# Second matrices of the wide layer: 512-column products made as two of 256 columns, and the row tiles moved by 128 bytes

## The chip, the cores and the metric

One core of a Trainium2 chip runs the whole program. The metric is the device time in microseconds. The kernel before took 1237.65 us (median of three runs, 1237.44 to 1240.28).

## What is computed

The reference runs four layers over 256 positions of width 1024: an SSM layer, an attention layer, and two layers of a second block. Each layer of the second block ends in a wide (feed-forward) part with a hidden width of 2816:

```python
h = rms_norm_2(x, ln_ffn_pre[l])
f = (jax.nn.silu(h @ ffn_w_gate[l]) * (h @ ffn_w_up[l])) @ ffn_w_down[l]
x = x + rms_norm_2(f, ln_ffn_post[l])
```

The change touches `@ ffn_w_down[l]`, a product of 256 x 2816 by 2816 x 1024, once for each of two layers.

## The kernel before

All weights come as one stream of slots. A slot holds up to two k-tiles (128 rows of a matrix each) of one chunk, and a chunk is 512 columns wide in most matrices. SP issues one DMA for each slot into `weights_raw`. ACT rounds the slot to `weights_hi` (fp32r), DVE makes `weights_lo` = raw - hi, and TensorE forms each product as hi*hi + hi*lo + lo*hi, so three matmuls stand for one. The activations are split the same way: `act_F_hi`/`act_F_lo` for most matrices, `ffn_F_hi`/`ffn_F_lo` (22 k-tiles of 256 positions) for the down matrix.

There are two forms of this triple:

- **Rows held** (`tile_slot`, lines 705 to 707). 128 positions of the activation rows are the stationary operand (the weight load reads 128 of them) and 512 columns of the weight slot stream through. It is called for each of the two tiles of positions, writes `acc[par][t]`, a PSUM bank of 512 columns, and is used by nearly all matrices. Two chunks are 416 columns wide and four are 384, and their matmuls are as wide.
- **Weights held** (`hidden_slot`, lines 683 to 685). 128 columns of the weight slot are stationary and 256 positions of the activations stream through. It is used for the last two attention input chunks, the convolution input, and chunks 1 to 10 of the gate and up matrices of the wide layer.

The order on TensorE is written out by hand. In each wide layer it is: chunk 0 of gate/up with rows held, chunks 1 to 10 with weights held (960 matmuls, after the first 96 of which four transposes are put in), and then the down matrix: `down.0` slot by slot, `down.1` with seven slots so and the last four tile by tile (`by_tile(4, {})`). The down matrix has 22 k-tiles x 2 tiles of positions x 2 chunks x 3 = 264 matmuls of 512 columns for each layer. After it ACT squares the result (line 1284), POOL makes the root and DVE normalises.

SBUF tiles are placed in the order of the `sb(...)` calls, one after another, and some tiles lie over others that are dead by then. Between them stand unused tiles whose only effect is a shift. By these sizes `weights_hi`, `weights_lo` and their `_more` pairs begin 192 bytes past a multiple of 256. `act_F_*`, `mla_F_*`, `conv_F_*`, `attn_F_*` and `ffn_F_*` begin 128 bytes past one. A k-tile of 512 columns is 2048 bytes of a partition and one of 384 columns 1536, both multiples of 256. One of 416 columns is 1664 bytes, so the second k-tile of such a slot begins 64 bytes past a multiple of 256.

Of the kernel before, what the change touches and what calls it, by code (L numbers as in the profile page):

```python
# [8 lines left out]
F32 = mybir.dt.float32  # L9
# [6 lines left out]
P = 128  # L16
# [158 lines left out]
def build(nc, stream, consts, x_in, ssm_ab, ssm_ldt, ssm_bc, rows, qk_gain, positions, decay, conv_p, lat_gain, out):  # L175
# [17 lines left out]
    with ctx:  # L193
        def sb(name, shape, dt=F32, scope=None):
            return (scope or ctx).enter_context(nc.sbuf_tensor(name, shape, dt))
# [32 lines left out]
        for a in begins:  # L228
            for p in range(R, R + R_MORE):
                n = min(n for n in range(a + R, NS) if place[n] == p)  # L230
# [37 lines left out]
        with ExitStack() as s1:  # L268
# [4 lines left out]
            par = sb("ssm_par", [P, 20, Q], F32, s1)  # L273
# [43 lines left out]
            ao_lo = sb("attn_F_lo", [P, HEADS, SEQ], F32R, s2)  # L317

        with ExitStack() as s3:
            h2_hi = sb("ffn_F_hi", [P, HT, SEQ], F32R, s3)  # L320
            h2_lo = sb("ffn_F_lo", [P, HT, SEQ], F32R, s3)
            ffn_t = sb("ffn_tanh_F", [P, 2, 2 * SEQ], F32, s3)
            ffn_h = sb("ffn_hid_F", [P, 2, 2 * SEQ], F32, s3)
# [47 lines left out]
        acc = [[ctx.enter_context(nc.psum_tensor(f"acc{p}{t}", [P, 512], F32)) for t in range(TT)] for p in range(2)]  # L371
# [174 lines left out]
        def reader_of(name, t):  # L546

            l, kind, i = split_name(name)
            n = 2 * i + t + 1
            return {  # L550
                "ssm_in.": (u_copied, n) if i < 2 else (z_silu, n - 4),
                "glu.": ((glu_biased, 2 * t + i + 1) if name[0] != "L" else
                         (conv_a_copied, 2 * l + t + 1) if i == 0 else (conv_tanh_made, 2 * l + t + 1)),
                "ssm_out.": (x_updated, n), "attn_out.": (x_updated, 4 + 2 * t + i + 1),
                "attn_in.": (squares_made, 2 * QK_NO[i] + t + 1) if i < 4 else (v_copied, n - 8) if i < 6 else (attn_z_silu, n - 12),
                "lat.": (lat_copied, 2 * l + t + 1),
                "uq.": (mla_q_copied, 4 * l + n), "ukv.": (mla_v_copied, 4 * l + n),
                "ret.": ((ret_rope_read, 4 * l + n) if i < 2 else (ret_v_copied, 4 * l + n - 4) if i < 4
                         else (ret_g_silu, 4 * l + n - 8)),
                "gate.": (gate_tanh, 12 * l + n),  # L560
                "mla_o.": (mla_weighed, 4 * l + n), "conv_o.": (conv_weighed, 4 * l + n),
                "ret_o.": (ret_weighed, 4 * l + n),
                "out.": (mix_scaled, 4 * l + n), "down.": (ffn_scaled, 4 * l + n),
                "ffn.": (ffn0_hid, TT * l + t + 1) if i == 0 else (ffn_gated if t == 0 else ffn_hid, FFN_F * l + i),
            }[kind]
# [62 lines left out]
        def _(pe):  # L628
# [24 lines left out]
            def f_tiles(chunk):  # L653
                if ".uq." in chunk:
                    return c_hi, c_lo, 0
                if ".ukv." in chunk:
                    return c_hi, c_lo, QR // P
                if ".mla_o." in chunk:
                    return mo_hi, mo_lo, 0
                if ".down." in chunk:  # L660
                    return h2_hi, h2_lo, 0
                if ".conv_o." in chunk:
                    return cf_hi, cf_lo, 0
                if chunk.startswith("attn_out."):
                    return ao_hi, ao_lo, 0
                return f_hi, f_lo, 0
# [21 lines left out]
            def tile_slot(at, t):  # L688

                s = slots[at]  # L690
                c = table[s["chunk"]]
                par, w = c["par"], s["width"]
                hi, lo, k0 = f_tiles(s["chunk"])
                first, last = at == c["start"], at == c["end"] - 1
                if t == 0:
                    pe.wait_ge(lo_made, at + 1 - WHOLE)
                if first and acc_user[par]:
                    who, value = reader_of(acc_user[par], t)
                    pe.wait_ge(who, value)
                for kk in range(s["nk"]):  # L700
                    k = k0 + s["k"] + kk
                    wh, wl = (f(at, slice(kk * w, (kk + 1) * w)) for f in (high, low))
                    xh, xl = (f[:, k, t * P:(t + 1) * P] for f in (hi, lo))
                    o = acc[par][t][:, 0:w]
                    pe.matmul(o, xh, wh, start=first and kk == 0, stop=False)  # L705
                    pe.matmul(o, xh, wl, start=False, stop=False)  # L706
                    i = pe.matmul(o, xl, wh, start=False, stop=last and kk == s["nk"] - 1)  # L707
                return i

            def run(n):  # L710

                nonlocal pos
                for _ in range(n):
                    s = slots[pos]
                    c = table[s["chunk"]]
                    par = c["par"]
                    first, last = pos == c["start"], pos == c["end"] - 1
                    if pos < WHOLE:
                        i = whole_slot(s, par, first, last)
                    elif s["chunk"] in with_channels:  # L720
                        pe.wait_ge(lo_made, pos + 1 - WHOLE)
                        hi, lo, _ = f_tiles(s["chunk"])
                        i = hidden_slot(s, par, hi, lo, first, last)
                    else:
                        for t in range(TT):
                            i = tile_slot(pos, t)
                    i.then_inc(slot_used, 1)
                    acc_user[par] = s["chunk"]
                    pos += 1

            def by_tile(n, before):


                nonlocal pos
                a = pos
                for t in range(TT):
                    for j in range(n):
                        pos = a + j if t else a
                        for step in before.get((t, j), ()):
                            step()  # L740
                        name = slots[a + j]["chunk"]
                        i = tile_slot(a + j, t)
                        if t == TT - 1:
                            i.then_inc(slot_used, 1)
                        elif name in tiled and a + j == table[name]["end"] - 1:
                            i.then_inc(first_tile, 1)
                for j in range(n):
                    name = slots[a + j]["chunk"]
                    acc_user[table[name]["par"]] = name
                pos = a + n  # L750
# [72 lines left out]
            for n in range(DT // 2):  # L823
                c = table[slots[n]["chunk"]]
# [225 lines left out]
            for l in range(DEPTH2):  # L1050
# [43 lines left out]
                for t in range(TT):  # L1094
                    n = len(turn_at)
# [1748 lines left out]
```

## Time and profile before

| what | us |
|---|---|
| median of three runs | 1237.65 |
| lowest and highest | 1237.44, 1240.28 |
| the profiled execution, whole | 1240.36 |
| its span, first to last instruction | 1238.5 |
| TensorE busy in it | 1207.6 (98%) |
| weight loads busy | 1015.8 (82%) |
| DVE, ACT, POOL busy | 902.3, 638.7, 102.3 |

All times in rows are from the profiled execution. Of a matmul two things are read: its duration (from the first column in to the last result out; durations of neighbours overlap) and the distance from its start to the start of the next one, which is what it costs in a full stream. A row of `windows` gives, for each engine, the busy time and in brackets how many instructions touch the window. In a full stream the distance is therefore (length of the window + one duration) / count.

### The profile page before, as it was taken

How to read it: one execution, taken by the hardware profiler on the slowest of the kernel's cores; microseconds unless marked ns; L12 is line 12 of the kernel's file. 1: busy time of each engine (PE TensorE's matmuls, PEld its weight loads, DVE VectorE, ACT ScalarE, POOL GpSimd, SP SyncE). 2: the span in 40 equal slices, each digit the busy share in tenths (PEclk: the TensorE clock that was granted, in tenths of full speed). 3: DMA queues.
4: the chain of work that ended last, by engine and by line, in shares of the span. 5: the costliest groups of instructions: out<-in, count | busy, mean ns of one | idle time of the engine just before them, and what ended most of it. 6: DMA issues, size and time to landing. Idle time of an engine off the chain costs nothing.

```text
span 1238.5 us, 19034 instructions
## 1 busy us (share of the span) xinstructions
PE 1207.6 (98%) x7597; PEld 1015.8 (82%) x7597; DVE 902.3 (73%) x1463; ACT 638.7 (52%) x1034; POOL 102.3 (8%) x163
## 2 busy tenths in 40 slices
PE   7999999999999999999999999999999999999998
PEld 3566778887978888787999987988788787999986
DVE  7998867767598998687656555589998687665553
ACT  4334565575547665546434443556575535444441
POOL 6400011101000200201000001000200201000000
PEclk9999999999999999999999999999999999999999
DMA  7735566444565455355666664565445355556552
GB/s 253 210 103 178 200 210 191 152 130 154 162 202 166 151 160 188 124 179 170 208 187 187 187 190 155 174 217 171 154 153 180 139 174 170 188 195 196 191 194 75
DMA packets 71958, 215.68 MB, mean 174 GB/s; under 512 B 16256, under 2 KB 19744, under 8 KB 71744
## 3 DMA queue, kind: packets, MB, share of 16 engines
q1 hardware_dynamic: 65008, 206.37, 52.0%
q0 software_dynamic: 2112, 6.97, 1.9%
q10 hardware_dynamic: 4752, 1.14, 0.4%
q8 instruction: 60, 0.98, 0.3%
q14 instruction: 26, 0.21, 0.1%
HBM read 208.95 MB, written 3.15 MB: 171 GB/s over the span
## 4 chain that ended last, share of the span: by engine, by line
PE 82%; DVE 10%; ACT 5%; issue 2%; POOL 1%; DMA 0%; SPq 0%; DVEq 0%; POOLq 0%; ACTq 0%
PE acc L705 16%; PE acc L706 16%; PE acc L707 16%; PE acc L683 7%; PE acc L684 7%; PE acc L685 7%; PE acc L642 3%; DVE weights_lo L1780 2%; PE mixed L1020 1%; ACT junk L1284 1%; PE mixed L1117 1%; PE turned L760 1%; ACT weights_hi L1249 1%; DVE h_T L1810 1%; PE mixed L1004 1%
## 5 line engine op out<-in xcount | busy, mean ns | idle before, releaser
L1780 DVE TENSOR_TENSOR weights_lo<-weights_raw,weights_hi 128x1024 fp32r<-128x1024 f32 (+1 forms) x304 | 356.1, 1206 | 67.2 <-ACT weights_hi L1249 66.3
L1249 ACT ACTIVATE weights_hi<-weights_raw 128x1024 fp32r<-128x1024 f32 (+1 forms) x304 | 305.6, 1043 | 77.2 <-DMA weights_raw<-stream_dram 77.0
L705 PE MATMUL acc<-weights_hi,act_F_hi 128*128 128x512 f32 (+1 forms) x656 | 264.8, 404 | 4.2 <-DVE weights_lo L1780 2.5
L707 PE MATMUL acc<-weights_hi,act_F_lo 128*128 128x512 f32 (+1 forms) x656 | 256.7, 391 | 0.0
L706 PE MATMUL acc<-weights_lo,act_F_hi 128*128 128x512 f32 (+1 forms) x656 | 256.5, 391 | 0.0
L683 PE MATMUL acc<-act_F_hi,weights_hi 128*128 128x256 f32 x624 | 175.1, 281 | 0.0
L684 PE MATMUL acc<-act_F_hi,weights_lo 128*128 128x256 f32 x624 | 173.9, 279 | 0.0
L685 PE MATMUL acc<-act_F_lo,weights_hi 128*128 128x256 f32 x624 | 173.9, 279 | 0.0
L705 PEld LDWEIGHTS acc<-weights_hi,act_F_hi 128*128 128x128 f32 x656 | 123.6, 188 | 32.6 <-DVE weights_lo L1780 3.6
L707 PEld LDWEIGHTS acc<-weights_hi,act_F_lo 128*128 128x128 f32 x656 | 123.4, 188 | 26.8
L706 PEld LDWEIGHTS acc<-weights_lo,act_F_hi 128*128 128x128 f32 x656 | 123.7, 189 | 24.0
L685 PEld LDWEIGHTS acc<-act_F_lo,weights_hi 128*128 128x128 f32 x624 | 118.3, 190 | 0.0
L683 PEld LDWEIGHTS acc<-act_F_hi,weights_hi 128*128 128x128 f32 x624 | 117.3, 188 | 0.2
L684 PEld LDWEIGHTS acc<-act_F_hi,weights_lo 128*128 128x128 f32 x624 | 117.3, 188 | 0.2
L1810 DVE SCALAR_TENSOR_TENSOR conv_acc_F<-conv_in_F,conv_params,conv_acc_F 128x256 f32<-128x256 f32 x240 | 98.0, 480 | 0.0
L1780 DVE TENSOR_TENSOR weights_lo_more<-weights_raw_more,weights_hi_more 128x1024 fp32r<-128x1024 f32 (+1 forms) x60 | 71.5, 1215 | 18.0 <-ACT weights_hi_more L1249 17.8
L1810 DVE SCALAR_TENSOR_TENSOR ffn_tanh_F<-ffn_tanh_F,acc 128x512 f32<-128x512 f32 (+1 forms) x24 | 15.4, 642 | 93.4 <-ACT ffn_tanh_F L1369 88.8
L1249 ACT ACTIVATE weights_hi_more<-weights_raw_more 128x1024 fp32r<-128x1024 f32 (+1 forms) x60 | 61.6, 1048 | 26.0 <-DMA weights_raw_more<-stream_dram 25.8
L1369 ACT ACTIVATE ffn_tanh_F<-acc 128x512 f32<-128x512 f32 x20 | 12.0, 598 | 119.1 <-PE acc L685 119.1
L642 PE MATMUL acc<-weights_raw,hn_F 128*128 128x512 f32 x128 | 59.1, 609 | 1.2 <-DMA weights_raw<-stream_dram 1.2
L683 PE MATMUL acc<-act_F_hi,weights_hi_more 128*128 128x256 f32 x208 | 58.2, 280 | 0.0
L684 PE MATMUL acc<-act_F_hi,weights_lo_more 128*128 128x256 f32 x208 | 57.9, 279 | 0.0
(351 smaller groups left out, 1969.6 us busy)
## 6 DMA issues: line engine op xcount, KB each, us to landing
weights_raw<-stream_dram SPq DMA_DIRECT2D x306, 512.0 KB, 3.6
weights_raw_more<-stream_dram SPq DMA_DIRECT2D x58, 512.0 KB, 3.6
gains<-rows_dram POOLq DMA_DIRECT2D x12, 512.0 KB, 4.7
weights_raw<-stream_dram SPq DMA_DIRECT2D x6, 416.0 KB, 3.1
weights_raw<-stream_dram SPq DMA_DIRECT2D x4, 384.0 KB, 3.9
x_T<-x_in_dram SPq DMA_DIRECT2D x4, 256.0 KB, 6.4
ssm_bc<-ssm_bc_dram SPq DMA_DIRECT2D x1, 1024.0 KB, 8.1
u_scratch<-u_T ACTq DMA_DIRECT2D x4, 256.0 KB, 6.2
```

What stands on the lines that cost most here:

```text
L642: i = pe.matmul(acc[par][t][:, 0:w], f0[:, k, t * P:(t + 1) * P], whole(pos, slice(kk * w, (kk + 1) * w)), start=first and kk == 0, stop=l ...
L683: pe.matmul(o, wh, hi[:, k, :], start=first and kk == 0 and m % 2 == 0, stop=False, skip_group_check=True)
L684: pe.matmul(o, wl, hi[:, k, :], start=False, stop=False, skip_group_check=True)
L685: i = pe.matmul(o, wh, lo[:, k, :], start=False, stop=last and kk == s["nk"] - 1, skip_group_check=True)
L705: pe.matmul(o, xh, wh, start=first and kk == 0, stop=False)
L706: pe.matmul(o, xh, wl, start=False, stop=False)
L707: i = pe.matmul(o, xl, wh, start=False, stop=last and kk == s["nk"] - 1)
L760: i = pe.transpose(turned_bank[n % 2][:, kk * P:(kk + 1) * P], src(t, 4 * half + kk), ident)
L1004: x = pe.transpose(b[0:dk, (2 * n + t) * P:(2 * n + t + 1) * P], src(t, i), ident)
L1249: act.activation(high(s, slice(0, n)), whole(s, slice(0, n)), ACT.Copy).then_inc(hi_made, 1)
L1780: dve.tensor_tensor(low(s, slice(0, n)), whole(s, slice(0, n)), high(s, slice(0, n)).bitcast(F32), ALU.subtract).then_inc(lo_made, 1)
L1810: return dve.scalar_tensor_tensor(out=o, in0=a, scalar=s, in1=b, op0=op0, op1=op1)
```

## The change

In `tile_slot`, for chunks of the down matrix alone, each matmul of 512 columns becomes two of 256: first the three products of the left half, then the three of the right half, into the two halves of the same PSUM bank. Only the first matmul of the chunk's bank carries `start`, and only the last one `stop`. And an unused tile of 32 fp32 (128 bytes) ahead of `ffn_F_hi` moves `ffn_F_hi`, `ffn_F_lo`, `ffn_tanh_F` and `ffn_hid_F` by 128 bytes, so that they begin at a multiple of 256 bytes.

```diff
         with ExitStack() as s3:
+            sb("ffn_rows_offset", [P, 32], F32, s3)
             h2_hi = sb("ffn_F_hi", [P, HT, SEQ], F32R, s3)
             h2_lo = sb("ffn_F_lo", [P, HT, SEQ], F32R, s3)
...
                     xh, xl = (f[:, k, t * P:(t + 1) * P] for f in (hi, lo))
-                    o = acc[par][t][:, 0:w]
-                    pe.matmul(o, xh, wh, start=first and kk == 0, stop=False)
-                    pe.matmul(o, xh, wl, start=False, stop=False)
-                    i = pe.matmul(o, xl, wh, start=False, stop=last and kk == s["nk"] - 1)
+                    parts = 2 if ".down." in s["chunk"] else 1
+                    n = w // parts
+                    for c in range(parts):
+                        cols = slice(c * n, (c + 1) * n)
+                        o = acc[par][t][:, cols]
+                        end = last and kk == s["nk"] - 1 and c == parts - 1
+                        pe.matmul(o, xh, wh[:, cols], start=first and kk == 0 and c == 0, stop=False, skip_group_check=parts > 1)
+                        pe.matmul(o, xh, wl[:, cols], start=False, stop=False, skip_group_check=parts > 1)
+                        i = pe.matmul(o, xl, wh[:, cols], start=False, stop=end, skip_group_check=parts > 1)
                 return i
```

## Rows read from the trace of the kernel before

**Rows 1.** The page: span, busy time of the engines, granted clock in 40 slices.
```profile
span 1238.5 us, 19034 instructions
PE 1207.6 (98%) x7597; PEld 1015.8 (82%) x7597; DVE 902.3 (73%) x1463; ACT 638.7 (52%) x1034; POOL 102.3 (8%) x163
PEclk9999999999999999999999999999999999999999
```

**Rows 2.** The page: the chain that ended last.
```profile
PE 82%; DVE 10%; ACT 5%; issue 2%; POOL 1%; DMA 0%; SPq 0%; DVEq 0%; POOLq 0%; ACTq 0%
```

**Rows 3.** Windows in full streams: weights held (two), then rows held in the down stages.
```profile
610.00:700.00 90.00, 90.00 (x767) 90.00 (x766) 51.26 (x56) 39.62 (x48) 0.00 (x0) 1.00 0.61 187
1080.00:1170.00 90.00, 90.00 (x797) 90.00 (x796) 53.54 (x58) 39.38 (x48) 0.00 (x0) 1.00 0.59 194
706.00:766.00 60.00, 60.00 (x263) 49.02 (x261) 31.65 (x32) 26.52 (x35) 1.70 (x4) 1.00 0.57 172
```

**Rows 4.** Timeline of TensorE: handover from gate/up to down, layer 0; the last.
```profile
705.37 0.28 PE L685 MATMUL acc<-act_F_lo,weights_hi_more 128*128 128x256 f32 x1
705.49 0.40 PE L705 MATMUL acc<-weights_hi,ffn_F_hi 128*128 128x512 f32 x1
...
765.71 0.39 PE L707 MATMUL acc<-weights_hi,ffn_F_lo 128*128 128x512 f32 x1
```

**Rows 5.** The same in layer 1; then ACT's first reader of the last product.
```profile
1172.12 0.28 PE L685 MATMUL acc<-act_F_lo,weights_hi_more 128*128 128x256 f32 x1
1172.23 0.39 PE L705 MATMUL acc<-weights_hi,ffn_F_hi 128*128 128x512 f32 x1
...
1232.43 0.40 PE L707 MATMUL acc<-weights_hi,ffn_F_lo 128*128 128x512 f32 x1
1232.86 0.60 ACT L1284 ACTIVATE junk<-acc 128x512 f32<-128x512 f32 x1 [4.81 <-PE acc L707]
```

**Rows 6.** Weight splits inside the down stage of layer 0 (groups by form).
```profile
L1780 DVE TENSOR_TENSOR weights_lo<-weights_raw,weights_hi 128x1024 fp32r<-128x1024 f32 x14 | 16.9, 1224 | 10.2 <-ACT weights_hi L1249 10.2
L1249 ACT ACTIVATE weights_hi<-weights_raw 128x1024 fp32r<-128x1024 f32 x14 | 14.5, 1054 | 12.5 <-DMA weights_raw<-stream_dram 12.5
```

**Rows 7.** Windows before and after the four transposes of each gate/up stage.
```profile
593.00:602.00 9.00, 9.00 (x82) 9.00 (x81) 6.41 (x8) 4.37 (x5) 0.00 (x0) 1.00 0.81 263
1063.00:1073.00 10.00, 10.00 (x87) 10.00 (x86) 6.31 (x8) 4.52 (x6) 0.00 (x0) 1.00 0.71 242
```

**Rows 8.** Timeline, 384 columns, rows held: first and last of 24 starts.
```profile
332.37 0.33 PE L705 MATMUL acc<-weights_hi,mla_F_hi 128*128 128x384 f32 x1
...
336.36 0.34 PE L707 MATMUL acc<-weights_hi,mla_F_lo 128*128 128x384 f32 x1
```

**Rows 9.** Timeline, 416 columns: first matmul of each k-tile, even, odd, even, odd, even.
```profile
305.38 0.35 PE L705 MATMUL acc<-weights_hi,act_F_hi 128*128 128x416 f32 x1
...
305.95 0.35 PE L705 MATMUL acc<-weights_hi,act_F_hi 128*128 128x416 f32 x1
...
306.51 0.35 PE L705 MATMUL acc<-weights_hi,act_F_hi 128*128 128x416 f32 x1
...
307.08 0.35 PE L705 MATMUL acc<-weights_hi,act_F_hi 128*128 128x416 f32 x1
...
307.64 0.35 PE L705 MATMUL acc<-weights_hi,act_F_hi 128*128 128x416 f32 x1
```

**Rows 10.** Timeline of the four transposes in layer 0, 128 columns each.
```profile
603.29 0.60 PE L1162 MATMUL mixed<-consts,ffn_hid_F 128*128 128x128 f32 x4
```

**Rows 11.** Timeline of weight loads, weights held, layer 1.
```profile
1089.96 0.19 PEld L684 LDWEIGHTS acc<-act_F_hi,weights_lo 128*128 128x128 f32 x1
1090.07 0.19 PEld L685 LDWEIGHTS acc<-act_F_lo,weights_hi 128*128 128x128 f32 x1
```

## The prediction

> **What bounds the kernel now.** I read the page first. TensorE is busy for 98% of the span at the full granted clock in every slice [rows 1], and the chain that ended last lies on it for 82% [rows 2]. The windows of the two down stages come next. In layer 0 TensorE has no idle time, while DVE is busy for 31.65 and ACT for 26.52 of 60 us [rows 3]. So a nanosecond more or less between two matmuls of these stages moves the end by as much. What must be read is not the duration of a matmul (0.39 us, overlapping) but the distance of starts. Layer 0 has 264 matmuls from 705.49 to 765.71, so 60.22 / 263 = 229.0 ns each [rows 4]. Layer 1 has 60.20 / 263 = 228.9 ns [rows 5]. Together the two stages cost 528 x 228.9 ns = 120.9 us.
>
> The same program has 256-column fp32r matmuls in a full stream right ahead of both down stages. The window 610 to 700 counts 767, so (90 + 0.28) / 767 = 117.7 ns. The window 1080 to 1170 counts 797, so 113.3 ns [rows 3]. Same code, same clock, no idle time in either: the stream has **two cadences**, and keeps one for a whole stage. Which one it takes is settled where the stream is broken. Ahead of the four transposes, layer 0 runs at (9 + 0.28) / 82 = 113.2 ns and layer 1 at (10 + 0.28) / 87 = 118.2 ns [rows 7]; behind them each has the other one [rows 3].
>
> **The change part by part.** *Halving.* 528 matmuls of 512 columns go, 1056 of 256 columns come, each with its own weight load, and no wait is added. At the fast cadence a layer costs 528 x 113.3 ns = 59.8 us against 264 x 228.9 = 60.4 us, a gain of 0.6 us. At the slow one it costs 528 x 117.7 = 62.1 us, a loss of 1.7 us. Both layers fast is -1.2 us, one of each +1.1 us, both slow +3.4 us.
>
> Those rows are of the other form (weights held), so the price is bounded from both sides with rows held. Upper side: 384 columns cost (336.36 - 332.37) / 23 = 173.5 ns [rows 8]. The granted clock is 1.00 of 2.4 GHz [rows 3], so 384 columns take 160 ns and the matmul carries 13.5 ns of its own; one of 512 carries 228.9 - 213.3 = 15.6 ns. If that toll is paid for each matmul whatever its width, a half costs 106.7 + 13.5 = 120 ns, the pair 240 ns, and the sum is 1056 x 120 - 120.9 = +5.9 us (with a toll of 15.6 ns, 122.3 ns and +8.3 us). Lower side: the four transposes, 128 columns and a weight load each, begin (0.60 - 0.27) / 3 = 110 ns apart [rows 10], and 256 columns need 106.7 ns at this clock. At 109 ns a half, the sum is 1056 x 109 - 120.9 = -5.8 us. I take the measured 256-column stream, since width and weight-load spacing (1089.96 to 1090.07, 0.11 us [rows 11]) are the ones that the change makes, and the toll seems to follow the width: 6.6 or 11 ns at 256, 13.5 at 384, 15.6 at 512.
>
> The Trainium skill, "TensorE: Matmul & The Clock Gate", section "Back-to-back issue gap", speaks against halving: warm, a matmul costs N / 2.4 + 2.5 ns, so a cut in two pays the fixed part once more. By that rule on both sides the change would cost 528 x 2.5 ns = 1.3 us. The rows disagree with its absolute numbers: 228.9 ns where it has 215.8, and 113.3 or 117.7 where it has 109.2.
>
> *The shift by 128 bytes.* The rows begin 128 bytes past a multiple of 256, the streamed weights 192 past. After the change the rows begin at 0, which is 64 ahead of the weights modulo 256, the distance that stationary and streamed operands have in the weights-held form (192 against 128). One place shows that such a distance counts. With 416 columns the streamed k-tile begins in turn at 192 and at 64. An even k-tile (three matmuls) takes 0.57 us and an odd one 0.56 [rows 9]: 305.38, 305.95, 306.51, 307.08, 307.64. The shorter one is at the distance that the change makes. So the shift should make the halves no worse than the weights-held stream. I cost it at nothing beside that cadence, between -0.01 / 3 us = -3 ns on each of 1056 matmuls (-3.5 us, most of the way to the 109 ns above) and the same with the other sign. ACT and DVE write and read the moved tiles off the path.
>
> *What else moves.* PSUM halves are disjoint and one `start` clears the bank. ACT reads the bank after the last matmul, which ends 0.40 us after its start, at 1232.83, and ACT starts at 1232.86 [rows 5]. With halves the last starts 0.11 us later and lasts 0.28, so the tail gains nothing. Feeding: a slot takes TensorE 12 x 0.229 = 2.75 us, and ACT and DVE need 1.05 and 1.22 us for it [rows 6]; the gate/up stage eats slots in 24 x 0.1133 = 2.72 us and its TensorE never idles [rows 3], so a faster stage finds its slots ready. If that cover were gone, a slot would cost at most DVE's 1.22 us beside 2.75, still hidden. The density of instructions is also that of gate/up, so I put no issue cost on it.
>
> *The base.* The profiled execution took 1240.36 us, 1.9 us around its span of 1238.5, and 2.7 us more than the median 1237.65. It had the slow cadence in the gate/up stage of layer 0. 864 matmuls x 4.4 ns = 3.8 us less 0.4 us for the 96 ahead of the transposes is about the distance between the runs at 1237.5 and the one at 1240.3. My reading, not shown, is that the median run is fast in both gate/up stages. The down stage follows each without a break (705.37 to 705.49 and 1172.12 to 1172.23 [rows 4, 5]), so I expect it to go on in the cadence it finds. By the profiled execution's own time the sum is then +1.7 - 0.6 = +1.1, 1241.5 us. For a run like the median it is -1.2, **1236.4 us**.
>
> **The rivals.**
> 1. *Forecast:* both down stages take the fast cadence, 1236.4 us. For it: the same distance modulo 256, and no break ahead. Against it: the operand that changes with each triple is now the rows, and the handover may throw the stream into the other cadence.
> 2. *One or both down stages slow:* 1237.65 + 1.1 = 1238.8, or + 3.4 = 1241.1 us. For it: the slow cadence held all of layer 0's stage.
> 3. *The toll is paid for each matmul with rows held, slower:* 120 ns a half, 1237.65 + 5.9 = 1243.5 us. For it: 384, 416 and 512 columns with rows held all carry 13 to 17 ns [rows 3, 8, 9], nearly independent of width, and only the weights-held form carries less. It decides once a half costs over 114.5 + 3.7 / 1056 us = 118 ns. Against it: none of those is 256 wide.
> 4. *The alignment removes the toll:* 109 ns a half, 1237.65 - 5.8 = 1231.9 us. For it: the odd k-tiles of 416 columns. Against it: they still carry 13 ns, and the weights-held stream has this same distance and is never under 113 ns. The page named above gives this price (109.2 ns) for a warm matmul of 256 columns.
> 5. *The dice of layer 1:* its gate/up stage falls into the slow cadence because the stages before it are shifted in time, and down goes with it: 864 x 4.4 ns = 3.8, and down 2.3 us more than in the forecast. That is 1242.5 us.
> 6. *The change does nothing:* a pair costs what the whole did and the shift does not count, 1237.65 us.
>
> **How the numbers follow.** Chances: forecast 0.32, rival 2 0.25, rival 3 0.22, rival 4 0.10, rival 5 0.06, rival 6 0.05. 0.3% is 3.7 us, so 1233.9 to 1241.4 is no change, about what a measurement of this kernel can tell. Within: forecast, rivals 2 and 6, 0.62. Slower: rivals 3 and 5, 0.28. Faster: rival 4, 0.10. The forecast and rival 2 span 1236.4 to 1241.1. The range reaches over rival 4 at the low end (1231.9) and rival 3 at the high end (1243.5, a little more for the larger toll): 1232 to 1244.
>
> **What would show each step right or wrong.** In the profile after: 1056 matmuls on the moved down lines with 256 columns, durations near 0.28 us. Windows inside the down stages count (60 + 0.28) / 0.1133 = 532 matmuls if fast, 512 if slow, 502 if the toll is paid twice, 553 if it is gone. The down stage lasts 59.8, 62.1, 63.4 or 57.6 us for these. TensorE stays without idle time in it. The windows of gate/up tell the dice apart from the change. I would be wrong if the halves settle in a cadence that no stream before has, or if TensorE waits for `weights_lo` in the down stage.

## The result, and the profile after

The changed kernel takes 1244.7 us (median of nine runs, 1240.59 to 1244.99) against 1237.77 (nine runs, 1237.18 to 1240.28): a ratio of 1.005, interval 1.0041 to 1.0059. It is 6.9 us slower, where 1236.4 was forecast and the range ended at 1244.

The tile declarations and the loop moved the lines: the rows-held triple is 711 to 713, the weights-held one 684 to 686. The page's groups of the down stages show that each matmul is now 256 columns wide, twice as many, 0.28 us each (columns: engine, operation, out<-in, shapes, count, busy us, mean ns, idle before):

```profile
L712 PE MATMUL acc<-weights_lo,ffn_F_hi 128*128 128x256 f32 x288 | 80.9, 281 | 0.0
L711 PE MATMUL acc<-weights_hi_more,ffn_F_hi 128*128 128x256 f32 x64 | 18.0, 281 | 0.0
```

Windows of the kernel after, in this order: gate/up and down of layer 0, gate/up and down of layer 1.

```profile
610.00:700.00 90.00, 90.00 (x797) 90.00 (x796) 54.67 (x59) 40.63 (x49) 0.00 (x0) 1.00 0.63 194
710.00:760.00 50.00, 50.00 (x427) 50.00 (x426) 23.77 (x22) 19.18 (x22) 0.00 (x0) 1.00 0.57 172
1080.00:1165.00 85.00, 85.00 (x752) 85.00 (x751) 49.67 (x55) 37.92 (x47) 0.00 (x0) 1.00 0.62 193
1180.00:1230.00 50.00, 50.00 (x427) 50.00 (x427) 19.34 (x18) 15.49 (x20) 0.20 (x1) 1.00 0.41 134
```

Both gate/up stages of this execution are fast, (90 + 0.28) / 797 = 113.3 ns as in the second window of [rows 3]. Both down stages are slow: (50 + 0.28) / 427 = 117.8 ns for a half, 235.5 ns for what took 228.9. And the halves did not go on in the cadence that they found. The timeline of the handover in layer 0, and the windows of 20 us just ahead of it and just behind it:

```profile
703.73 0.28 PE L686 MATMUL acc<-act_F_lo,weights_hi_more 128*128 128x256 f32 x1
703.85 0.28 PE L711 MATMUL acc<-weights_hi,ffn_F_hi 128*128 128x256 f32 x1
...
765.91 0.28 PE L713 MATMUL acc<-weights_hi,ffn_F_lo 128*128 128x256 f32 x1
```
```profile
683.00:703.00 20.00, 20.00 (x179) 20.00 (x178) 13.03 (x14) 9.23 (x11) 0.00 (x0) 1.00 0.66 192
704.10:724.10 20.00, 20.00 (x172) 20.00 (x171) 13.35 (x13) 10.69 (x12) 0.00 (x0) 1.00 0.62 186
```

That is 20.28 / 179 = 113.3 ns ahead and 20.28 / 172 = 117.9 ns behind, with no break between. From first to last start the stage takes 62.06 us, where [rows 4] have 60.22. With one more distance each it is 62.18 against 60.45, so 1.7 us are lost for each layer in the down stages, 3.5 of the 6.9. The profiled execution, at 1242.21, is also faster than the median, with both gate/up stages fast. What the usual execution loses beyond the down stages is not in this profile. It is not the clock: the seven runs from 1244.09 us on list a mean granted clock of 0.998, the two below them 0.997.

### The profile page after: what moved, and what is told of

Same layout as the page of the kernel before. It is cut to its first block, busy times and chain, and to the rows that moved or that the text cites. A ratio compares the mean times of both kernels' runs of the same rounds, so it can differ in the third digit from the quotient of the medians.

```text
span 1240.4 us, 20090 instructions
## 1 busy us (share of the span) xinstructions
PE 1209.4 (97%) x8125; PEld 1038.0 (84%) x8125; DVE 902.4 (73%) x1463; ACT 639.1 (52%) x1034; POOL 101.7 (8%) x163
## 4 chain that ended last, share of the span: by engine, by line
PE 82%; DVE 9%; ACT 5%; issue 2%; POOL 1%; DMA 1%; DVEq 0%; POOLq 0%; ACTq 0%
PE acc L711 16%; PE acc L713 16%; PE acc L712 16%; PE acc L685 7%; PE acc L684 7%; PE acc L686 7%; PE acc L643 3%; DVE weights_lo L1786 2%; PE mixed L1026 1%; PE mixed L1123 1%; ACT junk L1290 1%; ACT weights_hi L1255 1%; PE turned L766 1%; DVE h_T L1816 1%; PE mixed L1010 1%
## 5 line engine op out<-in xcount | busy, mean ns | idle before, releaser
L712 PE MATMUL acc<-weights_lo,ffn_F_hi 128*128 128x256 f32 x288 | 80.9, 281 | 0.0
L713 PE MATMUL acc<-weights_hi,ffn_F_lo 128*128 128x256 f32 x288 | 80.9, 281 | 0.0
L711 PE MATMUL acc<-weights_hi,ffn_F_hi 128*128 128x256 f32 x288 | 80.9, 281 | 0.0
```

The costliest lines, as they stand in the source:

```text
L711: pe.matmul(o, xh, wh[:, cols], start=first and kk == 0 and c == 0, stop=False, skip_group_check=parts > 1)
L712: pe.matmul(o, xh, wl[:, cols], start=False, stop=False, skip_group_check=parts > 1)
L713: i = pe.matmul(o, xl, wh[:, cols], start=False, stop=end, skip_group_check=parts > 1)
```

## Experiments

Three questions: is it the halves or the shift; what settles the cadence of the down stage; where do the other 3 us come from.

**e1: the shift alone.**
```diff
-                    parts = 2 if ".down." in s["chunk"] else 1
+                    parts = 1
```


> The 128-byte shift alone, no product halved. Theory A (the halves run at 117.7 ns each and the rest of the loss is a gate/up stage that fell into the slow cadence behind the halved down stage of layer 0): the down stages keep about 228.9 ns, and the time stays within 1 us of the kernel before (1237.8). Theory B (the moved tiles cost on their own, in the matmuls that read them or in ACT and DVE): 2 to 4 us slower, with the down matmuls over 229 ns apart or the chain of the evacuation longer. If the distance of the operands modulo 256 counts as the odd k-tiles of 416 columns suggest, the down matmuls come at 226.7 ns and the time is 1.2 us lower.

Median 1242.93 us (five runs, 1240.44 to 1244.76), ratio 1.0041 (1.0029 to 1.0053). The window in the down stage of layer 0:

```profile
710.00:760.00 50.00, 50.00 (x216) 40.27 (x215) 23.89 (x22) 19.41 (x22) 0.00 (x0) 1.00 0.58 172
```

(50 + 0.40) / 216 = 233.3 ns for a whole product, where the third window of [rows 3] gives 229. The expected drop to 226.7 is refuted, and Theory B's price is there: 4.4 ns x 528 = 2.3 us, without any halving. It is not the whole loss: the profiled run, at 1240.56, has both gate/up stages fast and is 3.3 us over the median 1237.26 of the kernel before that ran beside it, and the median run is 5.7 us over it. e4 and e6 below come back to the rest.

**e2 and e12: the halves alone.** The same kernel, twice.
```diff
-            sb("ffn_rows_offset", [P, 32], F32, s3)
```


> The products halved, the row tiles left where they were. Theory A with alignment without effect: halves at 117.7 ns, same time as the changed kernel (1244.7). If the slow cadence comes from the distance of the operands modulo 256, the halves come at another distance than 117.7 ns: 113.3 ns gives 4.6 us less than the changed kernel, 120 ns (the toll paid for each matmul) 2.4 us more.

> The halved products without the shift once more, for its time against the kernel before: both down stages at 113.3 ns when the gate/up stage ahead is fast, 1235.6 us (1.3 below the kernel before) in most runs; about one run in ten 6.1 or 12.2 us above, where one or both gate/up stages and the down stage behind them are slow.

e2: median 1235.71 us (twelve runs). e12: 1235.61 us (eleven runs, 1235.21 to 1237.61), ratio 0.9981 (0.997 to 0.9992). In e2 eleven runs lie from 1235.41 to 1237.3 and one at 1248.11, which leaves its ratio unclear (0.9983 to 1.0015). Window in the down stage of layer 0, e2:

```profile
710.00:760.00 50.00, 50.00 (x444) 50.00 (x443) 24.17 (x24) 19.52 (x25) 0.85 (x2) 1.00 0.56 172
```

(50 + 0.28) / 444 = 113.2 ns for a half, so the stage takes 528 x 0.1132 = 59.8 us against 60.4 before. Halving by itself does what was forecast, and it is a version that beats both kernels, the one before by 0.2% and the changed one by 0.7%. The shift turned its gain into a loss.

**e3 and e4: halved in one layer only**, with the shift.
```diff
-                    parts = 2 if ".down." in s["chunk"] else 1
+                    parts = 2 if s["chunk"].startswith("L1.down.") else 1
```


> Shift in place, halved in layer 1 alone, so that nothing before the last down stage is changed. Theory A: only the down stage of layer 1 is longer, 528 x 117.7 - 264 x 228.9 ns = 1.7 us, so 1239.5, and the gate/up stages keep the cadences that they have in the kernel before. Theory C (the halves cost 3.5 us for each layer by something that a single profile of the changed kernel did not show): 1241.3.

> Shift in place, halved in layer 0 alone. Theory A: the down stage of layer 0 is 1.7 us longer, and the gate/up stage of layer 1 behind it falls into the slow cadence in most runs, 3.4 to 3.8 us more: about 1243. Theory C (3.5 us for each layer by itself): 1241.3, with the gate/up stage of layer 1 at 113.3 ns.

e3 took 1241.98 us (six runs, in two groups: 1240.15 to 1240.46 and 1243.49 to 1244.58), e4 (`"L0.down."`) 1243.28 (twelve runs, 1239.02 to 1247.99). I had expected 1239.5 for e3 from a down stage of layer 0 that keeps 228.9 ns; the shift had made it 233.3 there. The expectation that a gate/up stage turns slow because of the halves ahead of it finds no support: e3 has an upper group although nothing ahead of its last down stage is halved. The 1243 us expected of e4 was met by its median with that reason behind it, so this is luck. The profile of e4 is of its slowest run, 1247.99 us. Gate/up and down of layer 0, then of layer 1:

```profile
610.00:700.00 90.00, 90.00 (x766) 90.00 (x766) 51.26 (x56) 39.06 (x48) 0.00 (x0) 1.00 0.62 187
711.00:761.00 50.00, 50.00 (x427) 50.00 (x426) 25.45 (x23) 20.72 (x24) 0.00 (x0) 1.00 0.59 181
1082.00:1172.00 90.00, 90.00 (x767) 90.00 (x766) 51.26 (x56) 38.81 (x48) 0.00 (x0) 1.00 0.60 187
1182.00:1232.00 50.00, 50.00 (x216) 40.42 (x215) 23.25 (x21) 19.17 (x22) 0.00 (x0) 1.00 0.47 147
```

The gate/up stages count 766 and 767 in 90 us, where that of layer 0 in the kernel after counts 797: 117.8 ns, so 864 x 4.5 ns = 3.9 us more in each. A slow gate/up stage is thus a second part of the loss. It is seen here in e4; that the usual run of the changed kernel holds one is read from its time, for no profile of such a run exists. From 1236.8 (e12 plus the 1.2 us that halving gains) the sum is 1.7 us for the halves of layer 0, 264 x 4.4 ns = 1.2 for the whole products of layer 1, and 7.8 for the two gate/up stages, together 1247.5; measured 1247.99.

**e5 and e6: the two moved pairs of tiles apart.** e5 puts another 128 bytes behind `ffn_F_lo`, so that only the rows change their place modulo 256; e6 has only that second gap.
```diff
             sb("ffn_rows_offset", [P, 32], F32, s3)
...
             h2_lo = sb("ffn_F_lo", [P, HT, SEQ], F32R, s3)
+            sb("ffn_work_offset", [P, 32], F32, s3)
```


> Products halved, ffn_F_hi and ffn_F_lo at a multiple of 256 bytes, but ffn_tanh_F and ffn_hid_F kept at 128 past one by a second gap. The changed kernel's loss has two parts by now: 3.4 us from halves at 117.7 ns in the down stages, and about 4 us in most runs from a gate/up stage at 117.7 ns. Theory D (the place of the rows sets the down cadence, the place of ffn_hid_F, which the four transposes in the middle of gate/up read, sets how often gate/up turns slow): halves at 117.7 ns and nearly all runs near 1240.4, none or few near 1244.5. Theory E (the gate/up cadence does not depend on ffn_hid_F): most runs near 1244.5 as with the change.

> Products halved, rows left 128 bytes past a multiple of 256, ffn_tanh_F and ffn_hid_F moved to a multiple of 256. The down stages keep 113.3 ns in both theories. Theory D: most runs near 1235.5 + 4 = 1239.5. Theory E: nearly all runs near 1235.5, as with no tile moved.

e5: 1241.09 us (twelve runs; nine from 1239.93 to 1241.65, three from 1243.73 to 1244.02). e6: 1239.21 us (twelve runs; six from 1235.28 to 1236.87, six from 1241.56 to 1243.31). Down windows of layer 0, e5 and then e6:

```profile
710.00:760.00 50.00, 50.00 (x427) 50.00 (x426) 22.47 (x21) 19.39 (x24) 0.32 (x2) 1.00 0.54 166
```
```profile
710.00:760.00 50.00, 50.00 (x444) 50.00 (x443) 24.17 (x23) 19.66 (x24) 0.86 (x2) 1.00 0.54 170
```

The rows' place sets the cadence of the down stage, 117.8 ns at 0 and 113.2 at 128. The time agrees: e5's median is 3.7 us over the 1237.44 of the kernel before beside it, and the down stages account for 3.5. The place of `ffn_tanh_F` and `ffn_hid_F` leaves the down stage alone in the profiled run of e6, which is one of the lower six, and puts half of the runs some 6 us up, where 4 was expected.

**e7 and e9: the rows at 64 and at 192**, the two other tiles kept at 128. e7:
```diff
-            sb("ffn_rows_offset", [P, 32], F32, s3)
+            sb("ffn_rows_offset", [P, 48], F32, s3)
...
+            sb("ffn_work_offset", [P, 16], F32, s3)
```


> Products halved, rows 64 bytes past a multiple of 256 (128 behind the streamed weights), the other two tiles as before. If only the distance of the two operands counts, and 64 behind is fast (113.3 ns) and 64 ahead slow (117.7 ns), a distance of 128 shows whether there are more levels than two: I expect 113.3 or 117.7 ns and rule out nothing between 109 and 122.

> Products halved, rows 192 bytes past a multiple of 256, which is the place of the streamed weights; the two other tiles as before. So far halves came at 113.3 ns with the rows at 128, 117.8 at 0 and 118.7 at 64. If 128 is the only good place: 117 to 119 ns and 62 to 62.6 us for a down stage. If the place counts by its distance from the weights (64 behind is good): the same, or better than 113.3 only if no distance is best.

e7 took 1242.14 us (five runs), e9 (gaps of 16 and 48) 1242.99 (two runs). Their down windows of layer 0:

```profile
710.00:760.00 50.00, 50.00 (x424) 50.00 (x423) 22.92 (x21) 18.19 (x21) 0.00 (x0) 1.00 0.56 171
```
```profile
710.00:760.00 50.00, 50.00 (x419) 50.00 (x418) 22.65 (x21) 17.92 (x21) 0.00 (x0) 1.00 0.57 170
```

118.6 and 120.0 ns. With the streamed weights at 192:

| rows past a multiple of 256 | half, ns | whole, ns | both down stages, halves |
|---|---|---|---|
| 128 | 113.2 | 228.9 | 119.5 us |
| 0 | 117.8 | 233.3 | 124.4 us |
| 64 | 118.6 | not run | 125.2 us |
| 192 | 120.0 | not run | 126.7 us |

(1056 times the price of a half.) Of the four places the change left the only good one. e9's 117 to 119 ns was missed by 1 ns. Over the kernel before beside them, e7 and e9 took 4.7 and 5.4 us more; the table gives 4.3 and 5.8. That the places repeat every 256 bytes was not tested: the rows were moved by 0, 64, 128 and 192 bytes alone, and the weights stayed where they were.

**e8: halves for every 512-column product with rows held**, no shift.
```diff
-                    parts = 2 if ".down." in s["chunk"] else 1
+                    parts = 2 if w == 512 else 1
```


> No shift, and every 512-column product with rows held in two halves, not only the down matrix. All such rows lie 128 bytes past a multiple of 256 as the down rows do. If the place makes the halves fast, each 512-column product of a full stream gains 2.2 ns as in the down stages: some 2340 others, of which the trace has about half in full streams, so 2.5 to 5 us less than with the down matrix alone (1235.6): 1231 to 1233. If halves are slow where the stream is broken after each slot (the head loops), the gain is lost there: 1235 or more.

1245.44 us (six runs, 1244.88 to 1249.95), 8 us slower than the kernel before, where 1231 to 1233 was hoped for and 1235 or more allowed. All these rows lie at 128, and yet one cadence does not hold. About the same 20 us of code in layer 0 and in layer 1:

```profile
532.00:552.00 20.00, 20.00 (x179) 20.00 (x178) 16.61 (x18) 9.00 (x9) 0.00 (x0) 1.00 0.61 195
1002.00:1022.00 20.00, 20.00 (x172) 20.00 (x172) 16.04 (x18) 8.99 (x9) 0.00 (x0) 1.00 0.55 183
```

113.3 and 117.9 ns. At 128 both cadences can occur, and most streams that begin behind a break took the slow one. The window 172 to 215, a full stream in which the kernel before has 228.4 ns for a whole product, reads:

```profile
172.00:215.00 43.00, 43.00 (x367) 43.00 (x366) 29.77 (x62) 22.39 (x30) 5.96 (x6) 1.00 0.65 221
```

(43 + 0.28) / 367 = 117.9 ns, 235.9 for the pair. The down stages of e8 stay at 113.2 behind fast gate/up stages. So in this program halves paid where they followed a fast stream without a break; behind a break some streams took the fast cadence too, but most did not.

e8 also has a handover that does not pass the cadence on. In each layer the end of chunk 0 of gate/up is now a stream of halves with the rows at 128, and the 96 weights-held matmuls follow it without a break. The timeline in layer 0:

```profile
591.42 0.28 PE L711 MATMUL acc<-weights_lo_more,act_F_hi 128*128 128x256 f32 x1
...
597.99 0.28 PE L712 MATMUL acc<-weights_hi_more,act_F_lo 128*128 128x256 f32 x1
598.11 0.28 PE L683 MATMUL acc<-act_F_hi,weights_hi 128*128 128x256 f32 x1
...
609.30 0.28 PE L685 MATMUL acc<-act_F_lo,weights_hi 128*128 128x256 f32 x1
```

59 distances from 591.42 to 598.11 make 113.4 ns, and 95 from there to 609.30 make 117.8. In layer 1 it is the other way round: 1061.50 to 1068.45 gives 117.8 ns, 1068.45 to 1079.22 gives 113.4. So the cadence can change where the form changes, not only at a break.

**e10, e11 and e16: the place of `ffn_tanh_F` and `ffn_hid_F` again.** e10 and e16 are one kernel: the kernel before, with only the second gap of e6. e11 is the halves with that gap at 64 bytes, so that these tiles lie at 192.


> No product halved, rows as before, only ffn_tanh_F and ffn_hid_F moved by 128 bytes. The down stages stay at 228.9 ns. Theory D (the place of ffn_hid_F sets how often a gate/up stage turns slow): half of the runs near 1237.2, the other half 3.8 us above, near 1241, where the kernel before has about one run in eight there. Theory E: the same spread as the kernel before. If a slow gate/up stage hands its cadence to halves alone, the upper group here is 3.8 us above the lower one and not 6.1 us, as with halves and the rows at 128.

> Products halved, rows as before at 128, ffn_tanh_F and ffn_hid_F at 192 past a multiple of 256. Down stages at 113.3 ns. If only the place 0 of ffn_hid_F is bad: 1235.5 in nine runs of ten. If any place but 128 is bad: half of the runs near 1241.6.

> Products whole, rows at 128, ffn_tanh_F and ffn_hid_F at a multiple of 256. With one gate/up stage at 117.7 ns the time is near 1241 and the down stage behind it still at 228.9 ns; a second cadence of the whole products, which would explain that the upper runs lay 5 us above the lower ones, would show as 231 ns or more.

e10: 1240.44 us (twelve runs, 1236.38 to 1246.4), ratio 1.0025 (1.0009 to 1.0041), with down stages as before, x220 in the window 710 to 760, 229 ns. No matmul of the wide layer's streams reads the tiles that moved; only the four transposes of [rows 10] do. e11: 1236.29 us (eleven runs, 1235.41 to 1237.83), ratio 0.9987 (0.9978 to 0.9996), no upper group. e16: 1239.89 us (eight runs, four below 1239 and four from 1240.95 to 1243.36).

Counted by time, a run is raised when it is 3.5 us or more above the fastest of its kernel (for the kernel before, of those that ran beside the same experiments):

| `ffn_hid_F` past a multiple of 256 | kernels | raised |
|---|---|---|
| 0 | after, e1, e3, e4, e6 and e13 to e15, e10 and e16 | 41 of 88 |
| 128 or 192 | e2 and e12, e5, e7, e8, e9, e11 | 6 of 59 |
| 128 | before | 11 of 114 |

Kernels that differ in this place alone: 7 of 9 raised in the changed kernel against 3 of 12 in e5; 14 of 36 in e6 and e13 to e15 against 1 of 23 in e2 and e12; 10 of 20 in e10 and e16 against the 11 of 114 of the kernel before. The count is rough at its edge: the profiled run of before (1240.36) has a slow stage and is not in it, and one of e14 (1238.79) has none and is. That one of ten becomes nearly one of two is beyond that. That such a run holds a slow gate/up stage is seen in one profile alone, that of e4 (1247.99 us); the profile before, with layer 0 slow, is 2.8 us over the fastest. The clock is not behind it: with the tiles at 0, 35 of the 41 raised runs and 40 of the 47 others list a mean clock of 0.997 or more.

**e13 to e15: the kernel of e6 three more times**, to catch a slow gate/up stage ahead of halves at 128.

> Products halved, rows at 128, ffn_tanh_F and ffn_hid_F at a multiple of 256: one more execution with its profile. Where its time is near 1242, one gate/up stage must show 117.7 ns in the profile. If the halves take over the cadence that they find, the down stage behind it shows 117.7 ns too (62.1 us); if their place alone decides, 113.3 ns (59.7 us).

> The same program in another execution: a gate/up stage at 117.7 ns has a down stage of halves at 117.7 ns behind it if they take over the cadence, at 113.3 ns if the place alone decides. A time near 1236 goes with both gate/up stages at 113.3 ns.

> As the run before it, in a third execution: half of them are expected to have at least one slow gate/up stage, and a time near 1236, 1242 or 1248 with none, one or two.

The profiled executions took 1235.33, 1238.79 and 1236.33 us, all with fast gate/up stages ahead of down stages at 113.3 ns, so none holds the case that was sought; e16's (1237.4) was fast as well. The times speak for an inherited cadence: with the rows at 128 and halves the upper group of e6 lies 6.5 us over the lower one (means 1242.5 and 1236.1) and e2's single raised run 12.1 us over the mean of its fellows, against 3.8 + 2.3 = 6.1 and 12.2 worked out ahead. But e10, whose whole products have nothing to inherit, has four runs 5.1 us over its lower five (means 1242.3 and 1237.2; 1239.3, 1245.83 and 1246.4 left out), where 3.8 was expected; the two fours of e16 lie 4.4 apart. And at the other handover, in e8, the cadence was not passed on. It stays open.

## Why the prediction was wrong

- *What bounds the kernel*: right. TensorE is without idle time in the down stages of every profiled run, and the nanoseconds per matmul came out in the time within 0.5 us where only the rows moved (e5, e7, e9). The reading that the median run of the kernel before has both gate/up stages fast fits e16, whose whole products take 229 ns as well: fast in both at 1237.4.
- *Halving*: right in size, at place 128; why a half with rows held costs what a fast weights-held matmul does was not tested. 113.2 ns and -1.2 us were forecast for the halves on their own, e12 measured 1235.61 beside 1237.55 (-1.9, with the runs' spread), e2 1235.71 beside 1237.26 (-1.5). Rival 3, the toll that is paid again in each half (120 ns), is refuted at place 128: a half there costs 113.2. Rival 4 (109 ns) occurred nowhere.
- *The shift*: **the step that failed.** It was costed at nothing. It costs 4.4 ns for each whole product and 4.6 for each half: 1056 x 4.6 = 4.9 us in the changed kernel, which turns a gain of 1.4 us into a loss of 3.5 (119.5 and 124.4 us against 120.9). I had reasoned from a distance modulo 256, taken from the weights-held form and from the two places of a 416-column k-tile [rows 9], where the streamed operand moved. Here the stationary one moves. The distance 64 ahead is the fast one there and a slow one here, so the distance alone is not the rule. The bound of 3 ns either way was too narrow, too: it came from one difference of 0.01 us between k-tiles whose starts are given to 0.01 us.
- *Inherited cadence*: wrong for the changed kernel. With the rows at 0 the halves run at 117.8 ns whatever comes ahead, behind fast gate/up stages in both layers of the kernel after and of e5, behind a slow one in e4. That rival 2 has the right number for the down stages, 3.4 us, is luck: it put the slow cadence down to the stage ahead, not to the place.
- *The dice of layer 1* (rival 5): the slow gate/up stage is real and costs 3.9 us, as worked out (3.8), but how often it comes goes with the place of `ffn_tanh_F` and `ffn_hid_F`, not with a shift in time by the stages before: e10 changes nothing but that place. I had said of these tiles that they are written and read off the path. That holds for ACT and DVE; the four transposes on TensorE read `ffn_hid_F`, and behind them the cadence holds for 864 matmuls. That it works through these transposes is argued, not shown: the two tiles were always moved together, and only one raised run has a profile.
- *The sum*: 1237.8 + 3.5 from the down stages + 3.9 from one slow gate/up stage is 1245.2, 0.5 over the measured median 1244.7. The two rivals were priced one by one, and the range reached for the larger of them. Both come from the same edit and, by the times, mostly occur together. The term of 3.9 is an inference from time for the usual run of the changed kernel.

The Trainium skill's price of a cut ("TensorE: Matmul & The Clock Gate", "Back-to-back issue gap": 2.5 ns more for each extra warm matmul, so +1.3 us as an estimate) is not borne out at place 128, where cutting gains 2.5 ns for each pair. At place 0 a pair costs 2.2 ns more than a whole product there (235.5 against 233.3). The prediction used that formula for a stream, while the page calls it the gap of an isolated matmul and gives about 131 ns for 512 columns in a stream of weight loads and matmuls; the 228.9 ns here agree with neither.

## What to carry to other kernels

Where TensorE streams fp32r without a break, read the distance of starts out of windows and not the durations: differences of 4 to 5 ns for each matmul were the result here. Treat an SBUF shift as an edit with its own price, run it alone, and list every instruction that reads a moved tile, those in a break of a stream too. And when one edit feeds two rivals, price them together.

## What the runs showed of the hardware

- Distances between starts of fp32r matmuls in a full stream take a few steady values that depend on where the stationary rows lie (the streamed weights at 192 past a multiple of 256): 113.2, 117.8, 118.6 or 120.0 ns for 256 columns with the stationary rows at 128, 0, 64 and 192, and 228.9 or 233.3 ns for 512 columns at 128 and 0. Moves of 0, 64, 128 and 192 bytes were run, none of 256.
- Besides, one and the same stream has two such values, 113.3 and 117.8 ns. It can change at a break, as at the transposes (ahead of them [rows 7], behind them [rows 3]), or where the form changes (e8), and was then kept for all 864 matmuls of a gate/up stage. Such a stage is 3.9 us longer in the one than in the other, which fits run times in groups some 4 us apart.
- The granted clock falls to half now and then in a break between stages. In the profiled execution of the kernel after, TensorE waited 1.66 us for DVE ahead of the transposes of layer 0's normalised rows and 0.74 us behind them, and then had 0.50 of its clock (third column from the end of the window's row), which is 1.2 GHz:

```profile
579.21 1.30 PE L766 MATMUL turned<-consts,h_T 128*128 128x128 f32 x8 [1.66 <-DVE h_T L1816]
581.25 0.79 PE L711 MATMUL acc<-weights_hi,act_F_hi 128*128 128x512 f32 x1 [0.74 <-DVE act_F_lo L1816]
```
```profile
581.30:583.50 2.20, 2.20 (x5) 1.76 (x6) 1.89 (x3) 0.85 (x3) 0.00 (x0) 0.50 0.08 32
```

  Five matmuls of 512 columns touch these 2.2 us, where a stream at the full clock has eleven. It does not set this execution apart from the lowest run, 1240.59, which lists the same mean clock, 0.997. e1's profiled execution had 0.50 at 769.2 to 771.8 too, and e11's and e14's, both with a mean clock of 0.995, had it at 579 to 584.5 and 580 to 586.
